# The forgetting branch's causal mask: from mask products on TensorE to a VectorE sum in two-piece score rows

## What is computed

```python
s = einsum('bqhd,bkhd->bhqk', qi, k) * scale
s = s + ci[..., None] - cum_k[:, :, None, :]      # cum: running sum of log forget gates
s = where(k_pos[None, :] <= q_pos[:, None], s, -inf)
p = softmax(s, axis=-1)
o = einsum('bhqk,bkhd->bqhd', p, v)
```

## Time and profile before

| | us |
|---|---|
| median of 3 runs | 1456.67 |
| the profiled execution, its time | 1452.32 |
| its span, first to last instruction | 1450.6 |
| PE busy | 1401.9 |
| VectorE (DVE) busy | 993.5 |
| ScalarE (ACT) busy | 546.3 |
| GpSimd (POOL) busy | 582.0 |

### The profile page before, as it was taken

One profiled execution on the slowest core, in us unless ns is written; L12 is line 12 of the kernel. 1 busy time (PEld: TensorE's weight loads), 2 busy tenths in 40 slices (PEclk: granted clock), 3 DMA queues, 4 the chain that ended last, 5 costly groups with the idle time before them and its releaser, 6 DMA issues.

```text
span 1450.6 us, 19821 instructions
## 1 busy us (share of the span) xinstructions
PE 1401.9 (97%) x6923; PEld 1146.8 (79%) x6932; DVE 993.5 (68%) x1421; ACT 546.3 (38%) x1115; POOL 582.0 (40%) x467
## 2 busy tenths in 40 slices
PE   4999998999999999999999999999999999999998
PEld 2898776777777888888888788888888888888886
DVE  4876777565663666676755786667776666697768
ACT  3611467455463000101343533333333333464443
POOL 1415845233145445334302226777777764100000
PEclk9999999999999999999999999999999999999999
DMA  9500021111303644444242234444444446876763
GB/s 350 145 15 15 24 81 41 55 37 52 117 23 105 172 116 145 116 117 131 87 159 89 73 117 136 129 128 126 130 131 133 145 145 209 296 242 194 250 232 116
DMA packets 174811, 185.69 MB, mean 128 GB/s; under 512 B 15904, under 2 KB 128648, under 8 KB 174096
## 3 DMA queue, kind: packets, MB, share of 16 engines
q1 hardware_dynamic: 168336, 178.87, 39.3%
q10 hardware_dynamic: 6400, 5.83, 1.2%
HBM read 148.98 MB, written 35.69 MB: 127 GB/s over the span
## 4 chain that ended last, share of the span: by engine, by line
PE 86%; DVE 7%; issue 2%; ACT 2%; DMA 1%; POOL 1%; SPq 1%; DVEq 0%; ACTq 0%; POOLq 0%
PE PS L1944 69%; PE PS L2073 8%; PE PS L2127 2%; PE PS L2154 2%; PE PS L2181 1%; PE PS L2182 1%; DMA wada<-in_w_ada_dram 1%; ACT pt_hi L1051 1%; DVE s_row L1490 1%; PE PS L1955 1%; DVE ada_acc L1352 1%; POOL s_row L872 1%; DVE rope_b L1425 1%; DVE mx L1471 1%; DVE pt_lo L1514 1%
## 5 line engine op out<-in xcount | busy, mean ns | idle before, releaser
L918 POOL TENSOR_TENSOR ws_lo<-s_tmp,ws_hi 128x512 fp32r<-128x512 f32 x76 | 116.4, 1531 | 87.7 <-ACT ws_hi L1204 87.7
L1514 DVE TENSOR_TENSOR pt_lo<-PS,pt_hi 128x512 fp32r<-128x512 f32 (+3 forms) x128 | 74.5, 582 | 84.4 <-ACT pt_hi L1051 84.0
L1944 PE MATMUL PS<-T_hi,ws_hi 128*128 128x512 f32 x320 | 124.5, 389 | 0.0
L1944 PE MATMUL PS<-T_lo,ws_hi 128*128 128x512 f32 x320 | 124.5, 389 | 0.0
L1944 PE MATMUL PS<-T_hi,ws_lo 128*128 128x512 f32 x320 | 124.5, 389 | 0.0
L1944 PE MATMUL PS<-db_hi,da_hi 128*128 128x512 f32 x308 | 119.8, 389 | 0.0
L1944 PE MATMUL PS<-db_lo,da_hi 128*128 128x512 f32 x308 | 119.8, 389 | 0.0
L1944 PE MATMUL PS<-db_hi,da_lo 128*128 128x512 f32 x308 | 119.8, 389 | 0.0
L1944 PE MATMUL PS<-act_hi,w_hi 128*128 128x512 f32 x288 | 113.1, 393 | 0.8 <-DVE w_lo L1746 0.8
L1944 PE MATMUL PS<-act_hi,w_lo 128*128 128x512 f32 x288 | 112.2, 389 | 0.0
L1944 PE MATMUL PS<-act_lo,w_hi 128*128 128x512 f32 x288 | 112.1, 389 | 0.0
(11 more groups left out here) (318 smaller groups left out, 3718.0 us busy)
## 6 DMA issues: line engine op xcount, KB each, us to landing
dn_raw<-ff_dram SPq DMA_DIRECT2D x66, 256.0 KB, 4.3
adaraw<-in_w_ada_dram SPq DMA_DIRECT2D x32, 512.0 KB, 4.0
wraw<-in_w_in_dram SPq DMA_DIRECT2D x25, 512.0 KB
wraw<-in_w_ffn_in_dram SPq DMA_DIRECT2D x24, 512.0 KB, 5.0
ff_dram<-sl SPq DMA_DIRECT2D x22, 512.0 KB, 6.1
w2t<-in_w_ffn_out_dram SPq DMA_DIRECT2D x22, 512.0 KB, 6.8
w2sum_dram<-w2s SPq DMA_DIRECT2D x11, 1024.0 KB, 5.8
dn_raw<-w2sum_dram SPq DMA_DIRECT2D x44, 256.0 KB, 4.5
```

The lines of the kernel that those rows point to most:

```text
L918: pool.tensor_tensor(ws_hl[i][1][:, :, :], left(par, i), ws_hl[i][0][:, :, :].bitcast(F32), ALU.subtract)\
L1514: nc.vector.tensor_tensor(pt_hl[gp % 3][1][:, 0:n], PS[:, 4 + gp % 2, 0:n], pt_hl[gp % 3][0][:, 0:n].bitcast(F32), ALU.subtract).then_inc( ...
L1944: ins = nc.tensor.matmul(out_ap, lhs[a], rhs[b], start=first and i == 0, stop=last and i == 2)
```

## The change

The mask products go. In their place VectorE adds the mask to the gates of the diagonal tile, for both heads in one instruction of 256 columns, into a new tile `cs_diag`. Each row is then taken in two pieces for each head: the columns before the diagonal tile against `cs`, with the minimum into `nm_past`, and the diagonal tile against `cs_diag`, starting from `nm_past`, with the minimum into `nm`. The order is: mask sum, past piece of head 0, past piece of head 1, diagonal piece of head 0, diagonal piece of head 1. Row 0 has no past piece. `s_taken` is raised by the diagonal pieces. There are new waits of VectorE on its own `dve_step`, and on `s_taken` of the row before ahead of the mask sum.

```diff
+    nm_past = small("nm_past", [P, 2])
+    cs_diag = at("cs_diag", R0 + CS + 10 * KB, [P, 2, P])
...
+                past = w - P
+                if r > A_T:
+                    dve.wait_ge(s_taken, rows_taken(r))
+                nc.vector.tensor_tensor(cs_diag[:, :, :], cs[:, :, past:w], maskb[:, :, P:2 * P], ALU.add).then_inc(dve_step, 1)
+                step[0] += 1
+                made = [step[0], step[0]]
+                for h in range(2 if past else 0):
+                    nc.vector.tensor_tensor_reduce(out=s_row[i][:, h, 0:past], in0=src[h][:, 0:past], in1=cs[:, h, 0:past],
+                                                   scale=-SM, scalar=BIG, op0=ALU.add, op1=ALU.min,
+                                                   accum_out=nm_past[:, h:h + 1]).then_inc(dve_step, 1)
+                    step[0] += 1
+                    made[h] = step[0]
                 for h in range(2):
-                    ins = nc.vector.tensor_tensor_reduce(out=s_row[i][:, h], in0=src[h][:, 0:w], in1=cs[:, h, 0:w], scale=-SM,
-                                                         scalar=BIG, op0=ALU.add, op1=ALU.min,
-                                                         accum_out=nm[:, r % 4, h:h + 1])
-                    ins.then_inc(s_taken, 1)
+                    dve.wait_ge(dve_step, made[h])
+                    nc.vector.tensor_tensor_reduce(out=s_row[i][:, h, past:w], in0=src[h][:, past:w], in1=cs_diag[:, h],
+                                                   scale=-SM, scalar=nm_past[:, h:h + 1] if past else BIG, op0=ALU.add,
+                                                   op1=ALU.min, accum_out=nm[:, r % 4, h:h + 1]).then_inc(s_taken, 1)
...
-                                             kb_hl[pb % 2][y][rows, c0:c0 + n], start=(e == 0),
-                                             stop=(e == 2 and c0 + n < w))
-                for h in range(2):
-                    ins = nc.tensor.matmul(dst[h][:, w - P:w], identb[:, :], maskb[:, 0, P:2 * P], start=False, stop=True)
+                                                   kb_hl[pb % 2][y][rows, c0:c0 + n], start=(e == 0), stop=(e == 2))
```

More of the change, by code:

```diff
@@ L2126, in scores @@
                             rows = slice(h * HALF, (h + 1) * HALF)
-                            nc.tensor.matmul(dst[h][:, c0:c0 + n], qb_hl[pb % 2][x][rows, i * P:(i + 1) * P],
-                                             kb_hl[pb % 2][y][rows, c0:c0 + n], start=(e == 0),
-                                             stop=(e == 2 and c0 + n < w))
-                for h in range(2):
-                    ins = nc.tensor.matmul(dst[h][:, w - P:w], identb[:, :], maskb[:, 0, P:2 * P], start=False, stop=True)
+                            ins = nc.tensor.matmul(dst[h][:, c0:c0 + n], qb_hl[pb % 2][x][rows, i * P:(i + 1) * P],
+                                                   kb_hl[pb % 2][y][rows, c0:c0 + n], start=(e == 0), stop=(e == 2))
                 ins.then_inc(s_ready, 1)
```

## The result

The changed kernel takes 1468.50 us (median of 5 runs, 1465.11 to 1469.99) beside 1455.56 us for the kernel before. The ratio is 1.0093, with a 95% interval from 1.0078 to 1.0108: about 13 us slower. The forecast was slower, by 9.1 us, and 1465.8 us.

A forecast was written before the change was run, and what follows sets the result against it. It took a chain of PE's scores and VectorE's rows, up to the fills of step b + 5, to set branch B's pace. 7.8 + 0 + 1.3 = +9.1 us gave 1465.8 us; range 1460 to 1474.

The forecast's parts named there:

- What bounds it: In branch B, from row 4 to the fills of step b + 5, PE and VectorE form one chain with almost no slack.
- Rival 2: Fills of step b + 5 wait for something unseen, not head 0: +3.8 us, 1460.5; chance 0.10.
- What comes off PE: Two mask products fewer per row: 0.10 us where PE is the limit, VectorE's start 0.21 earlier where VectorE is.
- rival 3: The mask takes its array change along, 0.4 us a row: 1458.5, chance 0.09; faster form 1452, chance 0.05.
- The price of a piece: On VectorE, 1.04 ns a column plus 0.08 us an instruction; a 128-column piece 0.22 us, cutting a head 0.08.
- rival 1: Overlap on VectorE is gone, every short instruction stands alone: about +18 us, 1475; chance 0.14.
- The price of the mask sum: VectorE's sum of 256 columns costs 0.34 us a row, from a 0.424 us PSUM row less 0.08 overlap.
- The walk: Rows 4 to 7 of a pair: delays grow to +1.96 us at the fills of step b + 5, 7.8 for four pairs.
- Rows 0 to 3: Net 0 in pairs 1 to 3; +1.3 us in the first pair, bounds 0.5 and 2.5.
- The last pair: After row 7's scaling there is cover; in the last pair ScalarE is tighter, worth 0.1 us at most.
- upper bounds for a row: VectorE's extra cost of 1.0 us a row instead of 0.51, which brings the loss to +18 us.

The follow-up runs named there:

- e1: The changed kernel, but row 7 takes head 0 whole (past piece, diagonal piece) before head 1; 1462.9 us, ratio 1.0057 to the kernel before.
- e10: The kernel before without its mask products (mask left out), with GpSimd waiting until the last row is scaled; 1450.32 us, ratio 0.9972.
- e6: The kernel before without its 64 mask products and nothing in their place (mask left out); 1452.03 us, ratio 0.9988.
- e2: The changed kernel with the mask sum issued before VectorE waits for the row's scores; 1459.39 us, ratio 1.0040 to the kernel before.
- e11: The kernel before with only GpSimd's wait for the last scaling added, as a control; 1454.53 us, ratio 1.0000.

## Why the prediction was right, and where it was off

- **What bounds it.** Right. PE waits for VectorE at the rows and at the fills of step b + 5, the fills in each of the four pairs 0.14 or 0.15 behind head 0 (388.85 to 389.00), and at 375.67, 379.63 and 384.16 the scores stand 0.14 or 0.15 behind the minimum. Rival 2, that the fills wait for something else, fell with their four waits for nm; e1 moved just these.
- **What comes off PE.** Right: 0.12 for a row in e10, on average. The forecast had 0.10 where PE is the limit and 0.21 where VectorE is. The fill starts 0.25 after the last scores of 256 columns (376.67 to 376.92), where the mask started 0.22 after them and the fill 0.10 later. From the last scores to the fill that is 0.07 less, so the gap stays and merely moves to the fill, which is against both forms of rival 3 (they wanted 0.2 or more). The Trainium skill says ("TensorEngine Tiling (Array Packing)", Key Properties) that a change of the tiling mode drains TensorE. The trace agrees: the full-row fill comes 0.25 behind scores that stand 0.11 or 0.12 apart among themselves. Within branch B, PE's busy time falls by 1.9 us (193.10 to 191.20 over the stretches of 202.57 and 216.82 us named above). The page's total grows by 2.9: PE is busy 3.5 us more ahead of branch B, where the mean granted clock is 0.98 and was 0.99, and 1.3 more behind it. I should have named the stretch and not the total.
- **The price of a piece.** The term mis-sized first. A piece that takes its start value from `nm_past` lasts 0.34 to 0.35 and stands 0.27 from the next (374.89 to 375.17), where I had 0.22. I took the row of a piece with a constant; the new form had no row. It costs 0.05 more, 0.10 for a row. The waits that are already satisfied cost nothing, as forecast, so rival 1 did not come: the pieces overlap, and e1 shows that a wait for the instruction just before costs 0.11. The prediction let the Trainium skill speak for rival 1 by its rule that the next operation starts only when the pipe is empty. The same paragraph ("VectorE: DVE Perf Modes", The DRAIN you can't avoid) goes on that a next operation which is not held starts earlier. With that exception the page is no witness for rival 1, and the trace agrees: the next piece starts 0.07 before the end of one of 0.34.
- **The price of the mask sum.** The term mis-sized most. It is 0.35 in rows 4 and 5 (373.33 to 373.68), forecast 0.34, but 0.48 in row 6 and 0.66 in row 7. There GpSimd scales an earlier row:

```profile
379.86 1.58 POOL L874 TENSOR_SCALAR s_row<-s_row,rden 128x640 f32<-128x640 f32 x2 [7.93 <-DVE rden L1518]
385.37 1.97 POOL L874 TENSOR_SCALAR s_row<-s_row,rden 128x768 f32<-128x768 f32 x2 [3.93 <-DVE rden L1518]
```

  In row 6 the sum ends 0.28 us behind the second scaling (381.44 and 381.72), in row 7 as much behind the first (386.27 and 386.55): the same picture as in e6. My nearest row reads PSUM and has no GpSimd beside it. The past pieces behind it, which have one input in PSUM, keep their time (0.94 and 1.08).
- **The walk.** Rows 4 to 7 took 2.19, 2.46, 2.85 and, to head 0, 3.03 us on VectorE; forecast 2.08, 2.35, 2.62 and 2.67. These are 0.11, 0.11, 0.23 and 0.36 more, 0.8 together, and the fills lose 2.7 a pair rather than 1.96. On PE, against the start of row 4, row 5 loses 0.22, row 6 0.62 and row 7 1.15, forecast 0.12, 0.42 and 0.73. Against that I overlooked a gain. Before, the transposes of step b + 8 wait for the scaling of row 7, which ends at 382.94, and start 0.15 later at 383.09. After, they don't, and 0.24 come back. What remains is 2.4 a pair: 9.7 us instead of 7.8.
- **Rows 0 to 3.** Forecast 0 for pairs 1 to 3; measured 0.25 each, 0.75 together. Forecast 1.3 for the first pair; measured 2.06, inside its bounds of 0.5 and 2.5. PE's waits there grew at the lo half from 0.15 to 1.50 (252.15), and 0.67 for nm came in at 246.41; the wait for row 3 did not change (0.99, now 1.01).
- **The last pair.** A miss: "ScalarE is tighter, worth 0.1 at most". It costs 1.7, by the collision of the scaling with GpSimd. The trace of before already had it, 2.45 at 433.77 beside 1.75 in the third pair, and I had not asked why. Even the 1.75 has GpSimd beside it (a scaling from 379.74 to 381.75); alone it is 1.42.

The sum as measured is 9.7 + 1.7 + 0.75 + 2.06 = 14.2 us beside the forecast's 9.1. By the ratio the change costs about 13 us. Direction and mechanism were right and the size about a third too small; the range of 1460 to 1474 held the time, by its upper bounds for a row. That 1468.50 lies only 2.7 above 1465.8 is in part luck: the loss was 3.8 more than forecast, and the median of before came out 1.1 lower than the one that the forecast started from.

## What to carry to other kernels

An engine that is busy for 97% of the span can still wait in a chain with one that is busy for 68%. Work moved from the first to the second gains 0.1 us and loses the whole latency of the new instructions where they stand between two hand-overs, and which result is released first counts as much as the amount of work. Put work that doesn't need the awaited data ahead of the wait (e2), finish the result that another engine waits for first (e1), and price an instruction by a row with the same operands and the same neighbours on the other engines.

## What the runs showed of the hardware

- VectorE instructions that work on data in SBUF take longer beside GpSimd's, and end a fixed time behind the GpSimd instruction. Two scalings of 128x1024 take 1.42 us together when alone and 3.93 to 4.35 when GpSimd's cast comes first or with them, and they end 0.54 to 0.56 us after the GpSimd instruction in eleven traces. A sum of 256 columns takes 0.42 alone and 0.56 to 0.90 beside a GpSimd scaling, ending 0.27 or 0.28 behind it; a copy of 256 columns 0.29 and 0.83. The pieces that read PSUM keep their time (1.08 for 896 columns both ways). That the two engines take turns, and that SBUF is the reason, is argued from these distances and from which instructions are hit; no run changed the operands' place alone.
- GpSimd pays too: its cast takes 1.49 to 1.51 us where it starts 0.4 or 0.5 us after VectorE's scaling, 1.03 to 1.06 else; its subtraction 2.67 to 2.70 beside the scaling, 2.38 or 2.39 behind it.
- A `tensor_tensor_reduce` with its start value in memory is 0.06 us longer (0.344 mean for 56) than one with a constant (0.288 mean for 8).
- The granted clock after an idle time of PE differs between executions of nearly the same code (1.00, 0.77 and 0.66 in the 5 us from 235: before, after and e11). The kernel before and e11 are 2.9 us apart in their spans (1450.6 and 1453.5), and the scores of row 0 are already 3.1 apart (236.56 and 239.65). The difference comes at two places: e11 is 0.2 us behind at 199 us and 1.8 at 207, where its clock was 0.89 (190 to 200 us) and 0.94 (200 to 210) and that of before 1.00, and it loses the rest near 235. Each place costs some 1.5 us. The kernel after had both too. What decides it stays open.
